# Last block: sixteen attention turns of two heads, with the projections between them

## The chip, the cores and the metric

The kernel runs on one core of a Trainium2 chip. The metric is the device time of one execution in microseconds (us); less is better. TensorE (PE) multiplies, VectorE (DVE) and ScalarE (ACT) work elementwise, GpSimd (POOL) helps, SyncE (SP) issues the weight loads.

## The reference, cut to what matters

The model is a stack of four blocks and then a last block of another kind, on one sequence of 512 positions with 1024 features. Only the last block is touched. It has four mixers side by side, each of 256 features in 4 heads of 64:

```python
def forgetting_attention(q, k, v, log_f):
    ...
        logits = (jnp.einsum('bhqd,bhkd->bhqk', qb, k) * scale
                  + cb[..., None] - cum[:, :, None, :])
        logits = jnp.where(key_pos[None, :] <= q_pos[:, None], logits, -jnp.inf)
        return jnp.einsum('bhqk,bhkd->bhqd', jax.nn.softmax(logits, axis=-1), v)

def stick_breaking_attention(q, k, v):
    ...
        log_keep = jnp.where(mask, jax.nn.log_sigmoid(-z), 0.0)
        log_rest = lax.cumsum(log_keep, axis=3, reverse=True) - log_keep
        att = jnp.where(mask, jnp.exp(jax.nn.log_sigmoid(z) + log_rest), 0.0)
```

The third mixer is a linear recurrence with a 64x64 state per head (`rwkv7_time_mix`), the fourth a gated linear unit (`rg_lru`). Each result is multiplied by its gate, all four are put together and projected (`w_out`).

## The kernel before

Everything is in float32. A product with weights is made of three matmuls over rounded high and low parts (`gemm`). Weights come in units of 128x2048: SyncE loads a unit, ScalarE rounds its high part (`high`), VectorE makes the low part (`low`, an operation of 2.3 us), and TensorE uses 16 tiles of it. There are two raw and three rounded buffers.

Each engine has an order written out by hand, and engines meet by semaphores. Long chains (the recurrence) are generators in the list `bgs`: each call of `bg()` lets an engine do one more step of them, up to the next `yield`, at a place that is the same in the orders of all engines. `rwkv_tensor`, `rwkv_vector`, `rwkv_scalar`, `rwkv_gpsimd` hold these steps for a pair of heads (`pp`): preparation (decay, keys, bonus), four 64x64 products of chunks, four transposed tiles, five levels of a triangular inverse (a "split" product and two "crossed" ones each), three products more, a state loop of 8 chunks with two steps each, and a normalisation at the end. Half a step more or less on one engine is waited for by the others.

PSUM has eight banks: four in the ring `gb` for projections, values and attention outputs, four in `mb` for scores, transposes and all products of the recurrence. `take` gets the next bank that isn't held and waits until its last content was read.

The attention (`attend_tensor`, `attend_scalar`, `attend_vector`, `attend_others`; kind 0 forgetting, kind 1 stick-breaking) goes for each kind: the values of four tiles, then for each of two pairs of heads the q and the k projection (`proj_tensor`, 24 matmuls of 512 columns), and then eight scores, one head and one 128-row query tile each, in the order of `SEQ`: 512, 512, 384, 384, 256, 256, 128, 128 key columns. `steps` lays these over each other: at a step TensorE transposes the weights of a score two or three back, makes a new score, and multiplies an older one with the values, with a `bg()` behind the score and one behind the product. For kind 0 the score is followed by a second product of 4 rows (line 2669) that adds the negative cumulated forget gates of the keys (`cum`) from a one-hot column of `cst`:

```python
pmm(pe, b, h, b[:, 0:n], q_[r, 128 * x:128 * x + 128], k_[r, 0:n], True, kind == 1)
if kind == 0:
    pmm(pe, b, 2, b[:, 0:n], K.ident[64:68, 64 + hd:65 + hd].broadcast_to([4, 128]), X.cum[64:68, 0:n], False, True)
```

`pmm` counts each product and waits for the last one in the same bank when the row group changes. On VectorE a kind 0 score takes a bias and mask operation on the last 128 columns, a bias on the rest (lines 2788 and 2790), a maximum, its negation, and after ScalarE's exp a reciprocal and a scaling. A kind 1 score takes abs, exp, ln on ScalarE and five operations on VectorE (lines 2812 to 2822), one of them a scan, then a last exp on ScalarE. Between the first and the second pair of kind 0 stands `between`: the recurrence of heads pair 0 is finished, the three projections of pair 1 are made, and its recurrence is begun.

## Time and profile before

| | us |
|---|---|
| median of 3 runs | 3229.66 |
| lowest, highest | 3228.27, 3239.74 |
| the profiled execution | 3230.81 |
| its span, first to last instruction | 3229.0 |
| mean granted TensorE clock | 0.94 of full speed |

Busy shares of the span: TensorE 91%, its weight loads 74%, VectorE 48%, ScalarE 34%, GpSimd 7%. The last block begins near 2740 us, the attention part of it runs from 2846.4 to 3163.6, and then come the last projection, the norm and the output. Busy time of an engine is not time at its peak: a matmul at the lower clock is busy for longer. Matmuls in float32 leave two records each. Tile names in the rows: `hh_`, `hl_` are the block's input, `wh_`, `wl_` weights, `Fg_` holds q, k, values and two score buffers, `rraw_` a third, `R_` the recurrence's tiles, `ST_`, `SA_` its state, `htf_` the transposed weights, `cum_` the cumulated gates, `cst_` the identity, `ps` a PSUM bank.

### The profile page before, as it was taken

The numbers are of one execution on the slowest core, as the hardware profiler recorded it, in microseconds if no ns is written. First come the engines' busy times: TensorE is split into PE (matmuls) and PEld (weight loads), VectorE is DVE, ScalarE is ACT, GpSimd is POOL, SyncE is SP. The second block draws the span as 40 slices with busy tenths as digits, with TensorE's granted clock in tenths as the row PEclk, the third lists the DMA queues.
The fourth block names the chain that finished last, engine by engine and source line by source line (L and its number), as shares of the span: only waits on it lengthen the run. The fifth ranks groups of instructions, "written<-read, shape, count | busy, mean of one in ns | idle before, by whom it ended". The sixth has DMA issues, their size and how long they took to land.

```text
span 3229.0 us, 39111 instructions
## 1 busy us (share of the span) xinstructions
PE 2949.0 (91%) x15982; PEld 2381.0 (74%) x15982; DVE 1552.2 (48%) x2302; ACT 1088.7 (34%) x1665; POOL 235.3 (7%) x216
## 2 busy tenths in 40 slices
PE   6999997399999989989999799998999998898977
PEld 5787886377888787787787488887788886665745
DVE  5776763834434334534334554344543344534444
ACT  4332332343212225525445232222332223422233
POOL 2333220000000000000000300000100000100000
PEclk9999998799999989989999899999999999987868
DMA  3244547433443221121221322222122222111000
GB/s 112 88 146 154 169 128 233 165 121 105 130 118 117 78 98 53 53 96 65 82 82 69 131 92 98 98 91 79 66 92 104 92 92 86 53 40 40 15 26 27
DMA packets 109956, 305.40 MB, mean 95 GB/s; under 512 B 27488, under 2 KB 67872, under 8 KB 80464
## 3 DMA queue, kind: packets, MB, share of 16 engines
q1 hardware_dynamic: 104656, 281.40, 26.3%
q10 hardware_dynamic: 5120, 21.50, 1.8%
q8 instruction: 125, 2.05, 0.3%
q14 instruction: 55, 0.45, 0.0%
HBM read 265.20 MB, written 41.85 MB: 95 GB/s over the span
## 4 chain that ended last, share of the span: by engine, by line
PE 80%; DVE 8%; ACT 3%; issue 2%; POOL 1%; SPq 1%; DMA 1%; DVEq 0%; ACTq 0%; POOLq 0%
PE ps L94 79%; DVE s_ L121 2%; PE ps L99 1%; SPq L158 1%; DVE H_ L121 1%; DVE htf_ L135 1%; ACT htf_ L117 0%; ACT hh_ L117 0%; ACT wh_ L117 0%; DVE ol_ L121 0%; DVE Pm_ L121 0%; ACT R_ L117 0%; ACT PT_ L117 0%; DVE nmx_ L143 0%; DVE R_ L121 0%
## 5 line engine op out<-in xcount | busy, mean ns | idle before, releaser
L94 PE MATMUL ps<-hh_,wh_ 128*128 128x512 f32 x2184 | 869.3, 398 | 20.4 <-DVE hl_ L121 12.4
L94 PE MATMUL ps<-hl_,wh_ 128*128 128x512 f32 x2184 | 854.6, 391 | 0.0
L94 PE MATMUL ps<-hh_,wl_ 128*128 128x512 f32 x2184 | 854.1, 391 | 0.0
L121 DVE TENSOR_TENSOR wl_<-raw_,wh_ 128x2048 fp32r<-128x2048 f32 x209 | 480.5, 2299 | 548.1 <-ACT wh_ L117 548.1
L117 ACT ACTIVATE wh_<-raw_ 128x2048 fp32r<-128x2048 f32 x209 | 399.0, 1909 | 354.6 <-PE ps L94 339.7
L94 PEld LDWEIGHTS ps<-hh_,wh_ 128*128 128x128 f32 x2184 | 412.7, 189 | 120.8 <-DVE hl_ L121 11.1
L94 PEld LDWEIGHTS ps<-hh_,wl_ 128*128 128x128 f32 x2184 | 412.5, 189 | 87.7
L94 PEld LDWEIGHTS ps<-hl_,wh_ 128*128 128x128 f32 x2184 | 413.2, 189 | 86.5 <-issue 3.7
L94 PE MATMUL ps<-ah_,wl_ 128*128 128x512 f32 x704 | 279.5, 397 | 0.0
L94 PE MATMUL ps<-ah_,wh_ 128*128 128x512 f32 x704 | 278.3, 395 | 0.0
L94 PE MATMUL ps<-al_,wh_ 128*128 128x512 f32 x704 | 277.7, 395 | 0.0
L117 ACT ACTIVATE sg_<-sg_ 128x512 f32<-128x512 f32 x88 | 55.6, 632 | 305.2 <-DVE sg_ L121 305.1
L94 PEld LDWEIGHTS ps<-ah_,wh_ 128*128 128x128 f32 x704 | 132.1, 188 | 32.7 <-issue 1.3
L94 PEld LDWEIGHTS ps<-al_,wh_ 128*128 128x128 f32 x704 | 132.1, 188 | 32.5
L94 PEld LDWEIGHTS ps<-ah_,wl_ 128*128 128x128 f32 x704 | 132.0, 188 | 31.5
L94 PE MATMUL ps<-wh_,hh_ 128*128 128x256 f32 (+1 forms) x480 | 141.4, 295 | 14.6 <-POOL hl_ L121 8.7
L121 DVE TENSOR_TENSOR sg_<-sg_,ps 128x512 f32<-128x512 f32 x88 | 60.5, 688 | 171.1 <-PE ps L94 130.4
L94 PE MATMUL ps<-wl_,hh_ 128*128 128x256 f32 (+1 forms) x480 | 139.1, 290 | 0.0
L94 PE MATMUL ps<-wh_,hl_ 128*128 128x256 f32 (+1 forms) x480 | 139.0, 289 | 0.0
L117 ACT ACTIVATE ah_<-sg_ 128x512 fp32r<-128x512 f32 x88 | 55.6, 632 | 238.9 <-DVE sg_ L121 238.9
L121 DVE TENSOR_TENSOR x_<-x_,ps 128x512 f32<-128x512 f32 x96 | 65.7, 685 | 143.2 <-PE ps L94 143.2
L117 ACT ACTIVATE sq_<-x_ 128x512 f32<-128x512 f32 x70 | 44.2, 632 | 239.8 <-DVE x_ L121 231.8
(318 smaller groups left out, 3696.1 us busy)
## 6 DMA issues: line engine op xcount, KB each, us to landing
raw_<-in_w SPq DMA_DIRECT2D x209, 1024.0 KB, 4.9
sO<-s5ce_ SPq DMA_DIRECT2D x32, 256.0 KB, 3.7
sW<-s5wt_ SPq DMA_DIRECT2D x16, 512.0 KB, 3.8
sA<-os_ SPq DMA_DIRECT2D x24, 256.0 KB, 2.2
ol_<-sA SPq DMA_DIRECT2D x24, 256.0 KB, 3.6
sT<-sK SPq DMA_DIRECT2D x32, 128.0 KB, 3.4
wh_<-sO ACTq DMA_DIRECT2D x4, 1024.0 KB, 11.3
wl_<-sO ACTq DMA_DIRECT2D x4, 1024.0 KB, 13.1
```

The source lines that it names most:

```text
L94: return self.e.matmul(out, lhsT, rhs, start=start, stop=stop, skip_group_check=True)
L99: return self.e.transpose(out, a, ident)
L117: return self.e.activation(out, a, f, bias=bias, scale=scale)
L121: return Nothing() if self.e is None else self.e.tensor_tensor(out, a, b, op)
L135: return self.e.scalar_tensor_tensor(out=out, in0=a, scalar=s, in1=b, op0=op0, op1=op1)
L158: return Nothing() if self.e is None else self.e.dma_start(out, a)
```

## The change

- Both heads of a pair go together. There are 16 turns (4 pairs i by 4 query tiles, 512 to 128 columns) and three more to run dry. In turn t TensorE makes the products of turn t-3 (the two heads alternate over key blocks, to column halves 0 and 64 of the bank), the transposes of turn t-2, and two scores one behind the other (row halves 0 and 64, two banks), then one `bg()`, then `FILLS[t]` pieces of projections, then two `bg()`.
- The pieces are half a q or k projection (12 matmuls) or one value tile (24 matmuls of 256 columns): 16 of them in turns 0 to 11. Only the first values and the first pair's q and k stand ahead of the turns.
- `between` (three projections) stands at turn 4, the recurrence of pair 1 gets its steps from turn 4 on.
- The 4-row product behind each score is gone. Instead four broadcasts of a whole row of `cum` (4 rows, 512 columns) are made once, ScalarE copies them to SBUF (`four`: the tiles `sq0`, `sq1`, `rs`, `ssq`), and VectorE adds score, query's gate and key's gates in one operation over all columns, and the mask in a second one over 128 columns.
- VectorE does, in a turn: both heads' score operations, both heads' scaling (kind 0), one `bg()`, at turns 6, 10, 14, 18 the gating of a finished pair, the fill's part (weights' low part, k copy), two `bg()`. ScalarE: two copies of transposes, both heads' exp (or abs, exp, ln), `bg()`, in kind 1 the last exp of the turn before, fill, two `bg()`.
- In kind 1 both scores of a turn are held in their banks until the next turn (`hold=i > 1`).
- The q and k tiles have two buffers each, score buffers number four. The weight units of the last block are laid out in the new order of use. Three tiles that only the first stages use are given free.
- In `rwkv_vector` four `yield`s, one behind each of four evacuations, become two behind each second one.

The diff, cut to its core:

```diff
--- before.py
+++ after.py
         dv.mark("out", "r.m", pp, n)
-        yield
+        if n % 2:
+            yield
+            yield
     yield
...
+TURNS = 16
+FILLS = (1, 1, 1, 1, 1, 1, 1, 2, 1, 1, 2, 3) + (0,) * 7
+V_ORDER = (0, 1, 2, 3), (3, 2, 1, 0)
...
 def at_views(K):
...
+    q = [Fg[:, 0:512], X.lw[:, :, :].rearrange("p a b -> p (a b)")]
+    k = [Fg[:, 516:1028], X.k1[:, :]]
...
-    Pm = [Fg[:, 2056:2056 + 512], Fg[:, 2568:2568 + 512], X.raw[:, 0:512]]
+    Pm = [Fg[:, 2056:2056 + 512], Fg[:, 2568:2568 + 512], X.cum[:, :], X.Pm3[:, :]]
+    four = [K.sq[0][:, :], K.sq[1][:, :], K.rs[:, :], K.ssq[:, :]]
...
-    return Fg[:, 0:512], Fg[:, 516:1028], V, Pm, [K.sq[0], K.sq[1], K.rs], neg
+    return q, k, V, Pm, four, neg
+def turn(t, h):
+
+    x = 3 - t % 4
+    return 2 * t + h, t // 4, x, 128 * (x + 1), 2 * (t % 2) + h
+def fill(e, t):
+    for _ in range(FILLS[t]):
+        next(e.fills)
...
-                pmm(pe, b, h, b[:, 0:n], q_[r, 128 * x:128 * x + 128], k_[r, 0:n], True, kind == 1)
-                if kind == 0:
-                    hd = 2 * pp + h
-                    pe.wait_ge(*K.at("f.ncu"))
-                    pmm(pe, b, 2, b[:, 0:n], K.ident[64:68, 64 + hd:65 + hd].broadcast_to([4, 128]), X.cum[64:68, 0:n], False, True)
-                pe.mark("aS", q0 + score)
-                pe.bg()
...
+def heads_tensor(K, pe, i):
+
+    for name in ("pr.q", "pr.k"):
+        b = K.gb.take(name, i, hold=True)
+        pe.wait_ge(*K.after(pe, K.gb, name, i))
+        for ks in (range(4), range(4, 8)):
+            gemm_part(K, pe, b, lambda k: (K.hh[:, k, :], K.hl[:, k, :], ("h", 8, k)), 8, ks)
+            if ks[0]:
+                pe.mark(name, i)
+                pe.rows.pop(id(b), None)
+                K.gb.let(name, i)
+            yield
+def fills_of(K, e, heads, values):
+
+    yield from heads(K, e, 1)
+    yield from heads(K, e, 2)
+    yield from values(K, e, 1)
+    yield from heads(K, e, 3)
+def attend_tensor(K, pe, between):
+    X = K.mx
+    q_, k_, V, Pm, four, _ = at_views(K)
+    for hd in range(4):
+        b = take(K, pe, K.mb, "f.b", hd)
+        pe.wait_ge(*K.at("f.ncu"))
+        pe.mm(b, K.ident[64:68, 64 + hd:65 + hd].broadcast_to([4, 128]), X.cum[64:68, :], True, True).then_inc(*pe.up("f.b", hd))
+    for _ in values_tensor_2(K, pe, 0):
         pe.bg()
+    for _ in heads_tensor(K, pe, 0):
         pe.bg()
+    pe.fills = fills_of(K, pe, heads_tensor, values_tensor_2)
+    for t in range(TURNS + 3):
+        if t == 4:
+            between()
+        if 3 <= t:
+            i, n = turn(t - 3, 0)[1], (t - 3) % 4
+            if n == 0:
+                O = take(K, pe, K.gb, "aO", i, hold=True)
+            for h in range(2):
+                pe.wait_ge(*K.at("a2.PT", turn(t - 3, h)[0]))
+            pe.wait_ge(*K.at("out", "av", i // 2, 3))
+            x = turn(t - 3, 0)[2]
+            for kk in range(x + 1):
+                for h in range(2):
+                    c = 64 * (2 * (i % 2) + h)
+                    pmm(pe, O, 0, O[64 * h:64 * h + 64, 128 * x:128 * x + 128], V[:, kk, c:c + 64],
+                        K.htf[h][:, 128 * kk:128 * kk + 128], kk == 0, kk == x)
+            pe.mark("a2.w", t - 3)
+            if n == 3:
+                pe.mark("aO", i)
+                K.gb.let("aO", i)
+        if 2 <= t < TURNS + 2:
+            for h in range(2):
+                q, i, x, n, w = turn(t - 2, h)
+                b = take(K, pe, K.mb, "aT", q)
+                pe.wait_ge(*K.at("a2.P", q))
                 for kk in range(x + 1):
+                    m = pe.tr(b[:, 128 * kk:128 * kk + 128], Pm[w][:, 128 * kk:128 * kk + 128], K.ident)
+                m.then_inc(*pe.up("aT", q))
+        if t < TURNS:
+            if t > 8:
+                for h in range(2):
+                    K.mb.let("aS", turn(t - 1, h)[0])
+            for h in range(2):
+                q, i, x, n, w = turn(t, h)
                 r = slice(64 * h, 64 * h + 64)
+                b = take(K, pe, K.mb, "aS", q, hold=i > 1)
+                pe.wait_ge(*K.at("a2.q", i))
+                pe.wait_ge(*K.at("a2.k", i))
+                pe.mm(b[:, 0:n], q_[i % 2][r, 128 * x:128 * x + 128], k_[i % 2][r, 0:n], True, True).then_inc(*pe.up("aS", q))
+        elif t == TURNS:
+            for h in range(2):
+                K.mb.let("aS", turn(TURNS - 1, h)[0])
+        pe.bg()
+        fill(pe, t)
+        pe.bg()
+        pe.bg()
...
+def attend_scalar(K, ac, between):
+    X = K.mx
+    q_, k_, V, Pm, four, _ = at_views(K)
+    for hd in range(4):
+        ac.wait_ge(*K.at("f.b", hd))
+        ac.wait_ge(*K.at("y", 6))
+        ac.wait_ge(*K.at("y", 7))
+        ac.act(four[hd], K.mb["f.b", hd], ACT.Copy).then_inc(*ac.up("out", "f.b", hd))
+    for _ in values_scalar_2(K, ac, 0):
+        ac.bg()
+    for _ in heads_scalar(K, ac, 0):
+        ac.bg()
+    ac.fills = fills_of(K, ac, heads_scalar, values_scalar_2)
+
+    def sticks_end(t):
+        for h in range(2):
+            q, i, x, n, w = turn(t, h)
+            ac.wait_ge(*K.at("a2.lg", q))
+            ac.act(Pm[w][:, 0:n], Pm[w][:, 0:n], ACT.Exp).then_inc(*ac.up("a2.P", q))
+
+    for t in range(TURNS + 3):
+        if t == 4:
             between()
+        if 2 <= t < TURNS + 2:
+            for h in range(2):
+                q, i, x, n, w = turn(t - 2, h)
                 ac.wait_ge(*K.at("aT", q))
+                if t > 2:
+                    ac.wait_ge(*K.at("a2.w", t - 3))
+                ac.act(K.htf[h][:, 0:n], K.mb["aT", q][:, 0:n], ACT.Copy).then_inc(*ac.up("a2.PT", q))
                 ac.mark("out", "aT", q)
+        if t < TURNS:
+            for h in range(2):
+                q, i, x, n, w = turn(t, h)
+                if i < 2:
+                    ac.wait_ge(*K.at("a2.mx", q))
+                    ac.act(Pm[w][:, 0:n], Pm[w][:, 0:n], ACT.Exp, bias=X.rp[:, w:w + 1], accum=X.rp[:, 4 + w:5 + w]).then_inc(*ac.up("a2.ex", q))
+                else:
+                    e1 = four[w][:, 0:n]
                     ac.wait_ge(*K.at("aS", q))
+                    ac.wait_ge(*(K.at("a2.e1", q - 4) if q > 19 else K.at("a2.mx", 15)))
                     ac.act(e1, K.mb["aS", q][:, 0:n], ACT.Abs).then_inc(*ac.up())
                     ac.wait_ge(*ac.now())
                     ac.act(e1, e1, ACT.Exp, scale=-1.0).then_inc(*ac.up())
                     ac.wait_ge(*ac.now())
                     ac.act(e1, e1, ACT.Ln, bias=1.0).then_inc(*ac.up("a2.ln", q))
+        ac.bg()
+        if 8 < t <= TURNS:
+            sticks_end(t - 1)
+        fill(ac, t)
+        ac.bg()
+        ac.bg()
...
+def attend_vector(K, dv, between):
...
+    for _ in values_vector_2(K, dv, 0):
         dv.bg()
+    for _ in heads_vector(K, dv, 0):
         dv.bg()
+    dv.fills = fills_of(K, dv, heads_vector, values_vector_2)
+    for t in range(TURNS + 3):
+        if t == 4:
             between()
+        for h in range(2) if t < TURNS else ():
+            q, i, x, n, w = turn(t, h)
+            p, dg, b = Pm[w], slice(128 * x, n), K.mb["aS", q]
+            if i < 2:
+                hd = 2 * i + h
+                dv.wait_ge(*K.at("aS", q))
+                dv.wait_ge(*K.at("out", "f.b", 3))
+                if q > 3:
+                    dv.wait_ge(*K.at("aT", q - 4))
+                dv.stt(p[:, 0:n], b[:, 0:n], X.cq[:, x, hd:hd + 1], four[hd][:, 0:n], ALU.add, ALU.add).then_inc(*dv.up("out", "aS", q))
+                dv.wait_ge(*dv.now())
+                dv.tt(p[:, dg], p[:, dg], NEGC, ALU.add).then_inc(*dv.up())
+                dv.wait_ge(*dv.now())
+                dv.red(X.rp[:, w:w + 1], p[:, 0:n], ALU.max).then_inc(*dv.up())
+                dv.wait_ge(*dv.now())
+                dv.ts(X.rp[:, w:w + 1], X.rp[:, w:w + 1], -1.0, None, ALU.mult).then_inc(*dv.up("a2.mx", q))
+            else:
+                e1 = four[w][:, 0:n]
+                dv.wait_ge(*K.at("a2.ln", q))
+                dv.stt(e1, b[:, 0:n], 0.0, e1, ALU.max, ALU.add).then_inc(*dv.up())
+                dv.wait_ge(*dv.now())
+                dv.tt(e1[:, dg], e1[:, dg], ONS, ALU.mult).then_inc(*dv.up())
+                dv.wait_ge(*K.at("aT", q - 4))
+                dv.wait_ge(*dv.now())
+                dv.scan(p[:, 0:n][:, ::-1], K.ones[:, 0:1].broadcast_to([128, n]), e1[:, ::-1], 0.0,
+                        ALU.mult, ALU.subtract).then_inc(*dv.up("a2.e1", q))
+                dv.wait_ge(*dv.now())
+                dv.tt(p[:, 0:n], p[:, 0:n], b[:, 0:n], ALU.add).then_inc(*dv.up("out", "aS", q))
+                dv.wait_ge(*dv.now())
+                dv.tt(p[:, dg], p[:, dg], NEGS, ALU.add).then_inc(*dv.up("a2.lg", q))
+        for h in range(2) if t < 8 else ():
+            q, i, x, n, w = turn(t, h)
+            dv.wait_ge(*K.at("a2.ex", q))
+            dv.recip(X.rp[:, 4 + w:5 + w], X.rp[:, 4 + w:5 + w]).then_inc(*dv.up())
+            dv.wait_ge(*dv.now())
+            dv.ts(Pm[w][:, 0:n], Pm[w][:, 0:n], X.rp[:, 4 + w:5 + w], None, ALU.mult).then_inc(*dv.up("a2.P", q))
+        dv.bg()
+        if t > 3 and t % 4 == 2:
+            i = (t - 3) // 4
+            dv.wait_ge(*K.at("aO", i))
+            gated(K, dv, i, K.gb["aO", i])
+            dv.mark("out", "aO", i)
+        fill(dv, t)
+        dv.bg()
+        dv.bg()
+def attend_gpsimd(K, po, between):
+    for _ in range(8):
+        po.bg()
+    for t in range(TURNS + 3):
+        if t == 4:
+            between()
+        for _ in range(3):
+            po.bg()
...
+    sqk = qk(sq, sk)
     return np.concatenate([_units(_tiles(np.concatenate([low, rkv(0), lx], 1))), _units(_tiles(np.concatenate([fg, sg, rg, lg], 1))),
-                           v(fv), qk(fq, fk)[0:1], _units(_tiles(rkv(1))), qk(fq, fk)[1:2], v(sv), qk(sq, sk)])
+                           v(fv), qk(fq, fk), _units(_tiles(rkv(1))), sqk[0:1], v(sv), sqk[1:2]])
```

## Rows read from the trace of the kernel before

**Rows 1.** Windows view, stretches of the attention part: length, then busy us (instructions) per engine, clock, DMA.
```profile
core 0: us, PE busy (x) PEld busy (x) DVE busy (x) ACT busy (x) POOL busy (x), PEclk, DMA share, GB/s
2846.40:2882.40 36.00, 35.28 (x309) 29.78 (x309) 8.95 (x16) 6.82 (x9) 0.00 (x0) 0.91 0.17 59
2882.40:2938.20 55.80, 47.22 (x190) 25.22 (x188) 20.81 (x65) 12.30 (x30) 0.64 (x2) 0.59 0.00 1
2938.20:2957.00 18.80, 18.80 (x74) 15.32 (x74) 6.11 (x5) 3.56 (x3) 0.00 (x0) 0.87 0.16 57
2957.00:2985.50 28.50, 17.81 (x121) 11.73 (x119) 15.79 (x22) 11.10 (x14) 3.15 (x3) 0.88 0.21 74
2985.50:3043.10 57.60, 55.09 (x780) 39.47 (x780) 26.87 (x66) 14.50 (x37) 6.34 (x5) 0.82 0.01 2
3043.10:3077.00 33.90, 32.15 (x234) 26.57 (x233) 9.29 (x18) 5.43 (x7) 0.00 (x0) 0.95 0.17 62
3077.00:3126.00 49.00, 35.19 (x154) 20.40 (x153) 24.52 (x56) 20.49 (x45) 0.00 (x0) 0.55 0.00 1
3126.00:3137.90 11.90, 11.08 (x48) 8.84 (x48) 3.67 (x3) 1.89 (x2) 0.00 (x0) 1.00 0.23 88
3137.90:3163.60 25.70, 17.80 (x76) 10.59 (x76) 18.61 (x40) 16.94 (x40) 0.00 (x0) 0.73 0.00 1
```

**Rows 2.** Groups of instructions by form, 2846 to 3163.5, TensorE: the 4-row products.
```profile
L94 PE MATMUL ps<-cum_,cst_ 4*128 4x512 f32 x8 | 6.6, 914 | 0.2
```

**Rows 3.** Timeline, TensorE: start us, us, instruction; scores and 4-row products.
```profile
2882.39 1.12 PE L94 MATMUL ps<-Fg_ 64*128 64x512 f32 x2
2883.57 1.12 PE L94 MATMUL ps<-cum_,cst_ 4*128 4x512 f32 x2
...
2885.19 2.07 PE L94 MATMUL ps<-Fg_ 64*128 64x512 f32 x2
...
3137.96 1.74 PE L94 MATMUL ps<-Fg_ 64*128 64x512 f32 x6 [0.87 <-DVE Fg_ L139]
```

**Rows 4.** Timeline, TensorE: products with the values, and transposes.
```profile
2912.46 1.97 PE L94 MATMUL ps<-htf_,Fg_ 128*64 128x128 f32 x8
...
3001.17 0.60 PE L99 MATMUL ps<-cst_,rraw_ 128*128 128x128 f32 x4
...
3014.86 1.09 PE L94 MATMUL ps<-htf_,Fg_ 128*64 128x128 f32 x8
```

**Rows 5.** Timeline, TensorE: the recurrence's chunk products; crossed x64, split x32 at 3022.15.
```profile
2980.00 0.69 PE L94 MATMUL ps<-R_ 64*64 64x64 f32 x32 [0.62 <-DVE R_ L121]
...
3018.82 2.38 PE L94 MATMUL ps<-R_ 64*64 64x64 f32 x64
...
3022.15 1.15 PE L94 MATMUL ps<-R_ 64*64 64x64 f32 x32
```

**Rows 6.** Timeline, VectorE: first and last of a kind 0 and a kind 1 score, one scaling.
```profile
2884.73 0.35 DVE L135 SCALAR_TENSOR_TENSOR Fg_<-ps,cq_,c_ 128x128 f32<-128x128 f32 x1 [1.94 <-PE ps L94]
...
2886.36 0.15 DVE L128 TENSOR_SCALAR rp_<-rp_ 128x1 f32<-128x1 f32 x1
...
2997.04 0.49 DVE L128 TENSOR_SCALAR rraw_<-rraw_,rp_ 128x512 f32<-128x512 f32 x1
...
3141.04 0.69 DVE L135 SCALAR_TENSOR_TENSOR sq_<-ps,sq_ 128x512 f32<-128x512 f32 x1 [3.23 <-ACT sq_ L117]
...
3144.07 0.29 DVE L121 TENSOR_TENSOR Fg_<-Fg_,c_ 128x128 f32<-128x128 f32 x1
```

**Rows 7.** Timeline, ScalarE: exp of a kind 0 score; exp and ln of kind 1.
```profile
2887.84 0.72 ACT L116 ACTIVATE Fg_<-Fg_,rp_ 128x512 f32<-128x512 f32 x1
...
3139.72 1.29 ACT L117 ACTIVATE sq_<-sq_ 128x512 f32<-128x512 f32 x2
```

**Rows 8.** Timeline, VectorE: last multiplications of the preparation; two state steps.
```profile
2977.26 2.69 DVE L121 TENSOR_TENSOR R_<-R_ 128x512 f32<-128x512 f32 x4
...
3044.89 0.28 DVE L135 SCALAR_TENSOR_TENSOR SA_<-ps,R_ 64x128 f32<-64x128 f32 x1 [1.29 <-PE ps L94]
...
3045.70 0.21 DVE L121 TENSOR_TENSOR ST_<-ST_,ps 128x64 f32<-128x64 f32 x1
```

More of the change, by code:

```diff
@@ L2832, in attend_others @@
-def attend_others(K, e, kind, proj, between=None):
-    for t in range(4):
-        e.bg()
-        if t == 0 and proj is proj_sync:
-            load(K, e, e.unit + 3)
-    e.unit += 1
-    for pp in range(2):
-        for _ in range(2):
-            proj(K, e) if proj is proj_sync else proj(e)
-            e.bg()
-        for turn, score, finish, weigh in steps(kind, pp):
-            if score is not None:
-                e.bg()
-            if weigh is not None:
-                e.bg()
-        if between and pp == 0:
+        if t == 3:
+            dv.unit += 1
@@ L2849, in attend_others @@
             between()
+        fill(sp, t)
 def drain(e):
@@ L3372, in memory @@
         fourier_memory(K, st, 3)
+    first.close()
     X = K.mx = Place()
```

284 lines of the change are left out of this document (83 added, 201 removed).

## The prediction

> **What bounds the kernel now.** I read the page first: TensorE is busy for 91% of the span, but only the last block is touched. So I read the windows view, cut at the ends of the steps of the attention part [rows 1]. It lasts from 2846.4 to 3163.6, 317.2 us. The reader is to see three things there. In the stretches of values and projections (2846 to 2882, 2938 to 2957, 3043 to 3077, 3126 to 3138) TensorE is full and its clock is 0.87 to 1.00, so they can only move, not shrink. In the four attention stretches (55.8, 57.6, 49.0 and 25.7 us, 188 us together) the clock is 0.55 to 0.82 and other engines end the waits. From 2957.0 to 2985.5 the recurrence of heads pair 1 runs its serial preparation on VectorE and ScalarE, and TensorE is busy for 17.8 of 28.5 us. The change spreads three things over 16 turns: attention, q/k/v projections, recurrence steps. The question is whether a turn is shorter than what it replaces.
>
> **TensorE's part.** Removed: 16 forget-bias products. The four of 512 columns show 6.6 us [rows 2]; by columns the four widths make 6.6 x (1 + 0.75 + 0.5 + 0.25) = 16.5 us. Each also waits for the score before it: score to bias starts 1.18 us apart for 1.12 us of work at 2.4 GHz [rows 3]. Added: four such broadcasts at the start, back to back, 4 us.
> Scores pair up. Three scores of different row halves (512, 512, 384 columns) once stood together and took 1.74 us, while one alone takes 1.12 us, 2.07 at 1.2 GHz [rows 3]. By that a pair of 512 takes about 1.0 us instead of 2.3. The products are one head after the other now, eight records in 1.09 us (1.97 at 1.2 GHz) [rows 4]. No row shows 128x64 products of two column halves alternating. Bounds: no overlap (1.0 us per four key blocks and head, nothing gained) and full overlap (half). The nearest row is the recurrence's 64x64 products, where 32 records that use all four quadrants take 0.69 us and 64 that use two at a time 2.38 us [rows 5]: column halves do overlap. I take half. Four transposes take 0.60 us [rows 4], unchanged.
> At 2.4 GHz a turn thus has on TensorE, for 512 columns: products 0.9, transposes 1.2, scores 1.1. Over the four widths of a head pair: 2.3 + 2.4 + 2.4 = 7.1 us. A half projection is 12 matmuls, 2.75 us (48 in 11.1 us in the stretch to 3137.9, at clock 1.00 [rows 1]); a value tile 3.2 us is my estimate from the same view (the 36.0 us stretch less two projections and eight recurrence steps of 1.5, by four).
>
> **VectorE's part, which sets the turn.** In the first eight turns VectorE does both heads' bias, mask, maximum, then waits for ScalarE's exp and scales, and only then serves a recurrence step. From the first operation to the negated maximum it is 1.78 us at 512 columns [rows 6]. The new form (one 512-column operation from PSUM at 0.69, one 128-column at 0.29, instead of 0.35 chained to 0.61) adds 0.15, so 1.9. Both heads 3.8, the second exp and its read-out 1.1 (0.72 for the exp [rows 7]), scaling 0.5 plus reciprocal 0.2 [rows 6]: 5.6 us. For 384, 256, 128: 4.9, 4.2, 3.5. In the last eight, abs/exp/ln of the first head take 1.9 us on ScalarE (0.6 and 1.29 [rows 7]), then VectorE 3.2 us a head (3141.04 to 3144.36 [rows 6]), 6.4 for both, then 5.3, 4.2, 3.1.
> After that come the steps. A state step on VectorE and back is 0.8 us (3044.89 to 3045.70) plus 0.5 for the update [rows 8]. Two of a turn's three steps come after VectorE's attention, because TensorE's second needs VectorE's answer to the first: 2.2 us. The projection half hides under the attention on VectorE, as long as that takes over 2.75 us. So turn = products + transposes + scores + VectorE's attention + 2.2.
>
> **The sum**, in us, part by part:
> - Start: 36.0 [rows 1] + 4.0 for the broadcasts, which stand ahead of the values on TensorE: 40. Cover for ScalarE's four copies: the values.
> - Turns 0 to 3: 1.1+5.6+2.2, 0.8+4.9+2.2, 1.8+4.2+2.2, 2.3+3.5+2.2 = 33, + 2.3 for a weight cast in a fill ahead of the second step, + 3 for the recurrence's last mean and variance (two round trips), + 2 for TensorE at 1.2 GHz part of the time: 40. Two projections are inside.
> - Three recurrence projections at turn 4: 19 [rows 1].
> - Turn 4: the preparation. Now it takes from 2957.0 to the end of the last of four multiplications at 2979.95 [rows 8], 23.0 us, with projections under it. VectorE's attention for turn 4 now stands in the middle, 5.6, and the first products' evacuation follows, 1.4: 30.
> - Turn 5: 8. Turn 6: products, transposes, scores 2.1, the recurrence's 16 transposes 2.0, fill 2.75, product 1.15, two evacuations 1.4, split 1.15, evacuation 0.8, crossed 2.38 [rows 5]: 13.7, + 2 for low clock: 16.
> - Turn 7 (two fills): 2.4 + 1.15 + 5.9 + 2.4 + 0.9 + 1.15 = 14. Turn 8: 1.4 + 1.1 + 1.9 + 6.4 + 1.4 + 1.15 + 0.8 + 2.4 = 17. Turn 9: 12. Turn 10 (two fills, three products of 3.5) 14. Turn 11 (three fills, 8.2) 14: here TensorE sets the turn, not VectorE.
> - Turns 12 to 15, no fill: 14 + 11.5 + 10.4 + 9.2 = 45, + 5 for low clock: 50. End: 10.
> Sum 40+40+19+30+8+16+14+17+12+14+14+50+10 = 284, against 317.2: **-33 us**. Hidden and costed at nothing: SyncE's eight loads (same bytes, DMA share at most 0.23 [rows 1]), the moved yields in `rwkv_vector` (four before, four after), GpSimd's steps (same), the new tiles (memory of finished stages). If that cover went, a late load would show as ScalarE's cast waiting for a DMA.
> The profiled execution is 3230.8 us (span 3229.0); less 33 is 3197.6. The median of the three runs is 1.2 lower, so I say **3196**. A measurement of this kernel can tell about 0.5%, 16 us, from no change.
>
> **The range.** Fast ends (turn 4's attention overlaps ScalarE's parts, clock full): 39+35+17+26+6+13+12+14+10+12+12+43+8 = 247, which is 3160. Slow ends (clock 1.2 GHz in most turns): 24 more, see below, 3220; I go to 3226.
>
> **Rivals.**
> A, low clock. TensorE's clock is 0.59 and 0.55 in the stretches where only small products run, 1.00 in dense projections [rows 1]; after the stretch at 0.59 the next one begins low, at 0.87 in the mean. If a half projection per turn does not lift it, two groups' 7.1 us and the recurrence products of turns 6 to 10 (some 20 us, half as much again) cost 14 + 10 = 24 more: 3220, no measurable change. Against it: 2985 to 3043 kept 0.82 without any projection. The Trainium skill (TensorE: Matmul & The Clock Gate, HAM oscillation) says that dense bursts parted by waits each begin at the lower clock, and advises keeping dense work together; this change parts 16 pieces that now stand together, so by that page the time is this rival's. The rows above agree that a dense stretch behind a sparse one begins low.
> B, better overlap. The engines' orders leave more slack than my turn formula (fills take the round trips, VectorE's second head starts while TensorE transposes): 37 us less, 3160.
> C, pairing is only in the text: products and scores of two heads still run one after the other. Then 9.6 us of scores and 8.5 of products return, about 15 of it on the chain: 3211. Against: [rows 3, 5].
> D, slower. In the last eight turns two of the four small PSUM banks are held by the scores for a whole turn, so transposes, products and steps share two. If the first step of each turn then waits for a bank that is emptied only behind VectorE's attention, the fill is no longer covered (3.2 + 3.2 + 5.9 + 8.2 = 20), one more round trip comes per turn (8 x 1.8 = 14), the recurrence's products come on top (7), at low clock (12): 53 more, 3249. It decides once turns 5 to 15, which I have at 13.2 us in the mean, pass 17.7. Against: now, with three scores held, a state step at 3077 to 3126 passes between them.
>
> **Chances.** My forecast 0.52 (nearly all of it below 3213.5), A 0.17, B 0.18, C 0.07 (half below), D 0.06. Faster by over 0.5%: 0.50 + 0.18 + 0.04 = 0.72; within: 0.22; slower: 0.06.
>
> **What would show it.** Right: no product of `cum_` beside scores; score pairs of 512 columns starting within 0.1 us and done in about 1 us; product pairs in half the time; the loop of 19 turns with the three projections from the first score to the last product about 244 us; turn 4 the longest, with TensorE idle behind VectorE; turns 7, 10, 11 full on TensorE. Wrong: turns of equal length whatever the width (something else than VectorE's attention sets them), ScalarE waiting for weights, or TensorE waiting in `take` for a bank in turns 8 to 15.

## The result, and the profile after

The kernel after takes 3221.83 us (median of 8 runs, 3219.05 to 3226.67), the kernel before 3232.66 us (8 runs, 3228.27 to 3239.74): ratio 0.9968, 95% interval 0.9957 to 0.9979, 10 us less. The profiled execution has a span of 3218.3 us against 3229.0. Faster, but by 0.3%, where 1% was forecast.

One thing has to be said before small differences are read. All kernels of this study do the same work in their first 2840 us, and yet in the profiled executions the last 4x4 product of `cum_`, just ahead of the attention part, starts anywhere between 2842.5 and 2852.5 us. So beside the medians I give the **rest**: from that product to the end of the span. It is 383.2 us before (2845.74 to 3228.99) and 372.3 after (2845.97 to 3218.31): 10.9 less, all of it behind that product.

The windows view of after, cut at the starts of turns (first scores of turns 0, 4, 5, 7, 10, 11, 12 and 15), the columns as in [rows 1]:

```profile
core 0: us, PE busy (x) PEld busy (x) DVE busy (x) ACT busy (x) POOL busy (x), PEclk, DMA share, GB/s
2846.60:2889.00 42.40, 40.94 (x318) 31.53 (x318) 8.98 (x16) 9.21 (x13) 0.00 (x0) 0.88 0.14 51
2889.00:2948.00 59.00, 48.75 (x279) 35.21 (x278) 31.27 (x74) 18.01 (x31) 0.64 (x2) 0.88 0.12 41
2948.00:2982.10 34.10, 14.28 (x100) 8.07 (x98) 19.73 (x32) 12.08 (x18) 2.43 (x3) 0.70 0.14 53
2982.10:3007.30 25.20, 22.35 (x275) 18.07 (x274) 12.92 (x32) 7.37 (x19) 3.21 (x3) 0.86 0.01 2
3007.30:3055.20 47.90, 36.21 (x519) 31.05 (x518) 24.94 (x45) 16.35 (x34) 3.96 (x3) 0.86 0.07 23
3055.20:3078.20 23.00, 16.68 (x182) 13.81 (x180) 8.50 (x17) 7.77 (x16) 0.00 (x0) 0.85 0.13 46
3078.20:3092.60 14.40, 13.28 (x84) 9.92 (x84) 4.86 (x15) 3.58 (x11) 0.00 (x0) 0.95 0.00 1
3092.60:3136.90 44.30, 22.23 (x148) 14.09 (x148) 19.68 (x45) 13.71 (x30) 0.00 (x0) 0.54 0.00 1
3136.90:3153.30 16.40, 10.48 (x59) 5.79 (x58) 6.17 (x17) 6.97 (x20) 0.00 (x0) 0.62 0.00 0
```

The part lasts 306.7 us against 317.2. TensorE is nearly full at the start and in turns 5, 6, 7 and 11 (turn 7 alone: 12.18 of 13.4 us, clock 1.00); in turn 4 and in turns 12 to 14 it is busy for half the time or less, and the clock there is 0.70 and 0.54. The parts of the sum beside what they became (start of a turn: its first scores; the last column is the best kernel of this study):

| part | forecast | after | E12 |
|---|---|---|---|
| start | 40 | 42.4 | 40.9 |
| turns 0 to 3 and three projections | 59 | 59.1 | 54.0 |
| turn 4 | 30 | 34.1 | 28.5 |
| turn 5, 6, 7 | 8, 16, 14 | 6.8, 18.4, 13.4 | 9.3, 18.3, 10.7 |
| turn 8, 9 | 17, 12 | 19.9, 14.6 | 17.9, 11.0 |
| turn 10, 11 | 14, 14 | 22.9, 14.5 | 18.7, 13.7 |
| turns 12 to 15 and end | 60 | 60.6 | 42.5 |
| sum | 284 | 306.7 | 265.5 |

What the change does to single operations, from the timeline of TensorE after:

```profile
2847.34 5.69 PE L94 MATMUL ps<-cum_,cst_ 4*128 4x512 f32 x8 [1.15 <-DVE cum_ L128]
2918.29 1.09 PE L94 MATMUL ps<-htf_,Fg_ 128*64 128x128 f32 x16
2948.04 1.13 PE L94 MATMUL ps<-k_,lw_ 64*128 64x512 f32 x4
3074.79 1.97 PE L94 MATMUL ps<-htf_,Fg_ 128*64 128x128 f32 x16
3092.64 2.08 PE L94 MATMUL ps<-k_,lw_ 64*128 64x512 f32 x4
```

The four broadcasts cost 5.7 us and a wait of 1.15. Pairing is real: two heads' products, 16 records, take 1.09 us (1.97 at half clock), what 8 records of one head took before [rows 4]; two heads' scores of 512 columns take 1.13 (2.08), what one took [rows 3]. But the 8 records of before stood alone: when the same 16 go one head after the other without a pause, they take 1.58 us (E6), so alternating takes a third off them, not half.

How a late turn is spent, from the timeline of turn 12 after, all three engines in order of time, lines left out at the dots:

```profile
3092.64 2.08 PE L94 MATMUL ps<-k_,lw_ 64*128 64x512 f32 x4
3094.65 0.33 PE L94 MATMUL ps<-SA_,R_ 64*64 64x64 f32 x4
3094.75 0.60 ACT L117 ACTIVATE sq_<-ps 128x512 f32<-128x512 f32 x1 [1.73 <-PE ps L94]
3096.70 0.69 DVE L135 SCALAR_TENSOR_TENSOR sq_<-ps,sq_ 128x512 f32<-128x512 f32 x1 [5.75 <-ACT sq_ L117]
...
3103.32 0.21 DVE L121 TENSOR_TENSOR ST_<-ST_,ps 128x64 f32<-128x64 f32 x1
3103.56 0.28 DVE L135 SCALAR_TENSOR_TENSOR ST_<-ST_,pc_,R_ 128x64 f32<-128x64 f32 x1
3103.90 0.90 PE L94 MATMUL ps<-R_,ST_ 64*64 64x64 f32 x3 [8.64 <-DVE ST_ L135]
3105.52 0.29 DVE L135 SCALAR_TENSOR_TENSOR SA_<-ps,R_ 64x128 f32<-64x128 f32 x1 [1.67 <-PE ps L94]
3106.42 0.22 DVE L121 TENSOR_TENSOR ST_<-ST_,ps 128x64 f32<-128x64 f32 x1 [0.61 <-PE ps L94]
```

The products of the first step end at about 3095.3. VectorE stands idle 5.75 us for ScalarE, then does both heads' attention, and answers the step at 3103.3; TensorE has waited 8.64 us. Only then come steps two and three, and the next turn's scores stand behind them.

### The profile page after: what moved, and what is told of

It reads as the page before. It is cut to its first block, busy times and chain, and to the rows that moved or that the text cites. A ratio compares the mean times of both kernels' runs of the same rounds, so it can differ in the third digit from the quotient of the medians.

```text
span 3218.3 us, 39085 instructions
## 1 busy us (share of the span) xinstructions
PE 2904.1 (90%) x15958; PEld 2360.8 (73%) x15958; DVE 1555.4 (48%) x2306; ACT 1091.1 (34%) x1669; POOL 236.3 (7%) x216
## 4 chain that ended last, share of the span: by engine, by line
PE 79%; DVE 9%; ACT 4%; issue 2%; POOL 1%; SPq 1%; DMA 0%; DVEq 0%; ACTq 0%; POOLq 0%
PE ps L94 78%; DVE s_ L121 1%; PE ps L99 1%; SPq L158 1%; DVE htf_ L135 1%; DVE H_ L121 1%; ACT htf_ L117 1%; ACT wh_ L117 1%; DVE R_ L121 0%; ACT hh_ L117 0%; DVE Pm_ L121 0%; DVE wl_ L121 0%; ACT rs_ L117 0%; DVE ol_ L121 0%; DVE Fg_ L135 0%
## 6 DMA issues: line engine op xcount, KB each, us to landing
wl_<-sO ACTq DMA_DIRECT2D x4, 1024.0 KB, 13.9
```

## The experiments

Theory 1: a turn is a chain through VectorE, long because of what stands in its line ahead of a recurrence step (the attention, weight casts), and the gain of the change lies elsewhere. Rivals: TensorE's work or low clock sets the turns; pairing and order bring the gain. In the table stand the median, the ratio to the kernel before with its 95% interval, the rest in the profiled execution, and the loop, which goes from the first scores to the last value product. E7 has the edits of E2 and E5 together, and E9 to E12 build on it:

| run | median | ratio | rest | loop |
|---|---|---|---|---|
| after | 3221.8 | 0.9968 (0.9957 to 0.9979) | 372.3 | 264.3 |
| E1 late cast | 3221.3 | 0.9966 (0.9953 to 0.9978) | 372.1 | 262.3 |
| E2 steps first | 3197.1 | 0.9887 (0.9868 to 0.9905) | 348.6 | 239.8 |
| E3 fills in turn 4 | 3229.0 | 0.9981 (0.9972 to 0.9991) | 375.8 | 267.1 |
| E4 bias alone | 3219.3 | 0.9964 (0.9951 to 0.9976) | 372.9 | |
| E5 fills last | 3216.3 | 0.9960 (0.9947 to 0.9974) | 367.5 | 258.7 |
| E6 unpaired | 3226.6 | 0.9986 (0.9977 to 0.9995) | 377.8 | 269.1 |
| E7 both orders | 3195.6 | 0.9890 (0.9876 to 0.9904) | 341.6 | 235.0 |
| E8 dense work in waits | 3222.4 | 0.9976 (0.9964 to 0.9988) | 371.8 | 262.6 |
| E9 fills in waits | 3193.2 | 0.9874 (0.9857 to 0.9892) | 345.1 | 236.4 |
| E10 all steps first | 3197.5 | 0.9897 (0.9881 to 0.9914) | 346.5 | 238.1 |
| E11 one step first | 3186.3 | 0.9860 (0.9842 to 0.9878) | 338.1 | 230.0 |
| E12 all together | 3182.0 | 0.9842 (0.9823 to 0.9861) | 331.4 | 224.6 |

### E4: the bias alone, in the old order

The edit, cut to its core (ScalarE's four copies and the waits are left out):

```diff
@@ attend_tensor of before, kind 0, ahead of the values
+        for hd in range(4):
+            b = take(K, pe, K.mb, "f.b", hd)
+            pe.mm(b, K.ident[64:68, 64 + hd:65 + hd].broadcast_to([4, 128]), X.cum[64:68, :], True, True)...
@@ the scores
-                pmm(pe, b, h, b[:, 0:n], q_[...], k_[r, 0:n], True, kind == 1)
-                if kind == 0:
-                    pmm(pe, b, 2, b[:, 0:n], K.ident[...], X.cum[64:68, 0:n], False, True)
+                pmm(pe, b, h, b[:, 0:n], q_[...], k_[r, 0:n], True, True)
@@ attend_vector
-                    dv.stt(w[:, dg], b[:, dg], c, NEGC, ALU.add, ALU.add)
-                    dv.ts(w[:, 0:128 * x], b[:, 0:128 * x], c, None, ALU.add)
+                    dv.stt(w[:, 0:n], b[:, 0:n], c, four_of(K)[hd][:, 0:n], ALU.add, ALU.add)
+                    dv.tt(w[:, dg], w[:, dg], NEGC, ALU.add)
```

> The kernel before, with one part of the change alone: the forget bias by four broadcasts ahead of the values and an add of VectorE, the 16 forget-bias products gone; the order of work is as before. Theory 1 (part of what the change removes had not been on the path): the broadcasts cost their full 6 us at the start, where TensorE is full, and the removed products give back 5 to 10 of their 16.5 us: between 0 and 4 us less than before. Rival (the scores' products are on the path): 16.5 less 6 and 2.4 for VectorE's longer form, 8 us less than before. Second rival (all of it was covered): 6 to 8 us more than before.

Measured 3219.3 us, 10.3 less than before by the rest: as much as the whole change. Windows of its two attention stretches of the first kind:

```profile
2898.20:2945.00 46.80, 37.14 (x175) 21.91 (x173) 22.31 (x67) 12.35 (x30) 0.64 (x2) 0.58 0.00 0
2992.20:3041.00 48.80, 43.72 (x764) 34.60 (x764) 28.05 (x68) 14.39 (x37) 6.35 (x5) 0.90 0.01 2
```

They were 55.8 and 57.6 us [rows 1]: 9.0 and 8.8 less. The start, from the last 4x4 product to the first scores, grows from 36.7 to 45.8, and the stretch behind the second (3041.0 to 3073.4) is 1.5 shorter: together 10.2. (In E4 the broadcasts meet the half clock, 6.83 us, and the clock of the start is 0.85 against 0.91.) In the kernel before, the removed products keep TensorE busy for 10.2 and 8.3 us in these two stretches, 18.5 in all, part of them at half clock. 17.8 us came off, so they were almost wholly on the path (the clock of the second stretch also rose from 0.82 to 0.90, and no run parts its share). The first rival was right, and my middle guess of 5 to 10 us was too low. The other parts of the change (16 turns, pairing, projections between the turns) together gave nothing that can be measured: 0.6 us by the rest, and E4 is the faster by 2.6 us in the medians and by 2.2 in the rest too, once the start is taken out (45.8 us there, 43.0 after, for the lower clock).

### E6: pairing undone

```diff
-            for kk in range(x + 1):
-                for h in range(2):
+            for h in range(2):
+                for kk in range(x + 1):
```

> The kernel after, with the value products of a turn one head after the other (as before the change) instead of alternating. The traces show 16 records in 1.39 us paired, 8 in 1.09 of one head at 2.4 GHz, so unpaired they take 0.8 us more at four key blocks and 8 us more over the 16 turns on TensorE. Theory 1 (the chain of a turn goes through VectorE, with products ahead of the scores on it): all of it is on the path, 5 to 8 us more than after, 3228. Rival (products lie in TensorE's slack): within 2 us of after, and the pairing was worth nothing in time.

Two groups of value products of this run, at the full and at half clock:

```profile
2917.46 1.58 PE L94 MATMUL ps<-htf_,Fg_ 128*64 128x128 f32 x16
3077.40 2.85 PE L94 MATMUL ps<-htf_,Fg_ 128*64 128x128 f32 x16
```

Measured 5.5 us more by the rest, 4.8 by the medians: as theory 1 expects. The 16 groups of value products take 22.0 us of TensorE in sum, 16.9 in the kernel after, and the loop is 4.8 longer: they are on the path. The saving stands where a turn has four or three key blocks (16 records: 1.58 us unpaired, 1.09 paired; 12: 1.15 and 0.88); with two and one it is nothing (1.13 and 1.12, 0.44 and 0.44). Pairing the products is worth some 5 us, known to within a few (the intervals of E6 and after just touch). Since everything but the bias came to nothing measurable, the order of the 16 turns must have cost about as much as pairing gave, or somewhat more; that last step is a difference, not a run of its own.

### E2: two steps ahead of the attention, turns 8 to 15

```diff
+EARLY = range(8, 19)
@@ TensorE
         pe.bg()
+        if t in EARLY:
+            pe.bg()
         fill(pe, t)
@@ ScalarE and VectorE, ahead of the attention
+        if t in EARLY:
+            dv.bg()
+            dv.bg()
```

(and one step behind it instead of three; the gating of a pair's output stands ahead of the two steps, since a step takes its bank)

> The kernel after, in turns 8 to 15 with the first two of a turn's three recurrence steps ahead of the attention on VectorE and ScalarE (TensorE: both ahead of the fill). Theory 1 (the late steps set the turn): the two round trips fall into the 5 us in which VectorE waits for abs, exp and ln, and the next scores no longer wait for VectorE; turns 8 to 15 fall from 14 to 23 us each to 10 to 18, 20 us less in all, 3202. Rival (a turn is VectorE's and ScalarE's own work, or TensorE at low clock, whatever the order): within 3 us of the kernel after, 3219 to 3225.

Measured 3197.1: 24.7 us less than after by the medians, 23.7 by the rest. The turns became 17.2, 13.3, 18.2, 13.7, 10.7, 11.5, 9.5 and 13.9, 108.0 us against 132.5. This is the largest single effect found. The steps now run while ScalarE does abs, exp and ln; the timeline of turn 12 in this run:

```profile
3085.52 1.13 PE L94 MATMUL ps<-k_,lw_ 64*128 64x512 f32 x4 [0.25 <-ACT htf_ L117]
3086.99 0.22 DVE L121 TENSOR_TENSOR ST_<-ST_,ps 128x64 f32<-128x64 f32 x1 [2.79 <-PE ps L94]
3088.75 0.29 DVE L135 SCALAR_TENSOR_TENSOR SA_<-ps,R_ 64x128 f32<-64x128 f32 x1 [1.23 <-PE ps L94]
3089.08 0.69 DVE L135 SCALAR_TENSOR_TENSOR sq_<-ps,sq_ 128x512 f32<-128x512 f32 x1
...
3095.55 0.21 DVE L121 TENSOR_TENSOR ST_<-ST_,ps 128x64 f32<-128x64 f32 x1
3095.80 0.28 DVE L135 SCALAR_TENSOR_TENSOR ST_<-ST_,pc_,R_ 128x64 f32<-128x64 f32 x1
3095.82 0.47 PE L99 MATMUL ps<-cst_,Pm_ 128*128 128x128 f32 x1 [4.68 <-DVE ST_ L121]
```

VectorE answers the step 1.5 us after the scores began (10.7 in the kernel after), and its attention begins 3.6 us after them (4.1 there). The last line is a new wait, taken up in E10.

### E1 and E5: the weight casts

E1 moves one cast, that of turn 10, from the fill to the end of turn 16. E5 leaves each in its turn, but puts all of a fill's work on ScalarE and VectorE behind the third step:

```diff
-        fill(dv, t)
         dv.bg()
         dv.bg()
+        fill(dv, t)
```

> The kernel after, with one weight cast moved: the one that ScalarE and VectorE do inside turn 10's fill is done at the end of turn 16. Theory 1 (VectorE serves its steps too late): in turn 10 TensorE's fill is over when ScalarE starts the cast (3068.05), and VectorE's answer to the step waits for both halves of the cast, until 3072.28; without it turn 10 falls from 22.9 to about 18.5 us, 4 us less in all, 3218. Rival (TensorE's two fills and its clock set turn 10): turn 10 stays within 1 us, 3221 to 3222.

> The kernel after, with what ScalarE and VectorE do in a fill (weight casts, evacuations of q and k and of the values) behind all three recurrence steps of the turn instead of between them; TensorE's order as it was. Theory 1 (what stands ahead of a step on VectorE lengthens the turn): turn 10 loses the 3.5 us that the late cast gave, turn 4 the same (the cast stands between the preparation's steps at 2965.9 to 2970.1), turn 7 one to two; turn 11, whose third half projection is awaited by the next scores, gains 1 back: 7 us less than after, 3215. Rival (the casts only take the place of waits for TensorE): within 2 us of after.

Turn 10 in the kernel after, from the timelines of VectorE, TensorE and ScalarE:

```profile
3062.38 0.68 DVE L121 TENSOR_TENSOR G_<-G_,ps 128x512 f32<-128x512 f32 x1
3063.11 0.39 PE L94 MATMUL ps<-wh_,hh_ 128*128 128x256 f32 x1 [2.46 <-DVE G_ L121]
3068.05 1.91 ACT L117 ACTIVATE wh_<-raw_ 128x2048 fp32r<-128x2048 f32 x1
3069.99 2.29 DVE L121 TENSOR_TENSOR wl_<-raw_,wh_ 128x2048 fp32r<-128x2048 f32 x1 [6.94 <-ACT wh_ L117]
3072.25 0.11 DVE L155 MEMSET ST_<- 128x64 f32 x1
3072.50 0.62 PE L94 MATMUL ps<-R_,ST_ 64*64 64x64 f32 x3 [2.04 <-DVE ST_ L155]
```

The cast's slot comes free with TensorE's last value product, in the same fill; ScalarE casts at 3068.05, VectorE ends its half at 3072.28, and the zero state that the first state step needs is set behind it. Taking the cast away gives TensorE's 2.04 us of wait and 1.5 more, which goes with the clock: in the kernel after it falls to 0.50 behind that wait (3074.1 to 3077.2), in E1 it stays at 1.00, and the turn's last 16 products take 1.09 us in place of 1.97. In E1 turn 10 fell from 22.9 to 19.4 us (18.5 expected), but 3.3 us came back at the end: 1.5 in the last turns, since the cast now stood in ScalarE's line ahead of the last transposed weights (TensorE waits 1.94 us for them in place of 0.46), and 1.8 behind the last value product, where the output projection begins 0.8 us later and runs at the lower clock for longer (0.59 in its first 7 us, against 0.75). The whole gave nothing. A right mechanism, and a miss for the time. In E5 turn 4 fell from 34.1 to 30.5, turn 10 to 19.4, turn 11 by 0.8 where a loss was expected, and turns 12 to 15 by 1.7; turn 7, from which one to two were expected, kept its length (13.7 against 13.4), and turn 5 grew by 1.2. In all 4.8 us less by the rest, 5.5 by the medians, 7 expected. Turn 0 lost 1.3 and turns 1 to 3 gave 3.3 back, the latter not for their code: E7, with the same there, hasn't lost it (last section).

### E3 and E9: half projections into turn 4

E3 fills turn 4 with four halves behind the first step, on all engines; E9 does it on top of E7's orders, with TensorE's halves parted:

```diff
-FILLS = (1, 1, 1, 1, 1, 1, 1, 2, 1, 1, 2, 3) + (0,) * 7
+FILLS = (1, 1, 1, 1, 4, 0, 0, 1, 1, 1, 2, 3) + (0,) * 7
@@ E9 only, TensorE in turn 4: two halves, step, half, step, half, step
```

> The kernel after, with the three half projections of turns 5, 6 and 7 done in turn 4, where TensorE waits 8.9, 6.3 and 3.4 us for the recurrence's preparation (fills 4, 0, 0, 1 in place of 1, 1, 1, 2). Theory 1: turns 5 to 7 are set by VectorE's attention plus the steps behind it, so a fill is nearly covered there; turn 4 grows by at most 1 us, turns 5 to 7 lose 1 us each: 2 us less, 3220. Rival (TensorE's work sets turns 5 to 7, and its clock): the three halves, 2.75 us each and more at half clock, come off the path: 7 to 9 us less, 3214.

> Both orders of the run before this one, and the three half projections of turns 5 to 7 moved into turn 4 again, but TensorE does two ahead of the first step, one behind it and one behind the second, and ScalarE and VectorE evacuate behind the third. Theory 1 (the same move lost 3.4 us because VectorE stood 4.56 us before an evacuation with the preparation behind it; TensorE's own waits of 8.9, 2.9 and 3.4 us have room): turn 4 stays at 29.8 within 1 us and turns 5 to 7 lose 3 us as they did there: 3 us less from the last 4x4 product to the end (341.6 there). Rival (TensorE's added work sets turn 4 itself): turn 4 grows by 3 us or more and nothing is won.

E3 was slower than after, by 3.4 us in the rest and by 7.2 in the medians: both theories missed. Turns 5 to 7 lost 3.1 us in sum, turn 4 grew by 4.9. From its timeline:

```profile
2980.92 0.69 DVE L139 COPY Fg_<-ps 128x512 f32<-128x512 f32 x1 [4.56 <-PE ps L94]
2981.53 0.68 DVE L121 TENSOR_TENSOR R_<-R_ 128x512 f32<-128x512 f32 x1
```

VectorE waits 4.56 us for the fourth half, with the recurrence's preparation behind it in its line. That is theory 1's own mechanism, which I had failed to apply. In E9, with the evacuation behind the steps, turn 4 stays at 29.5 and turns 4 to 9 are 4.1 us shorter in sum than in E10, which has the same turns 0 to 3, and 3.1 shorter than in E7: expected 3. By the rest E9 stands 3.5 us above E7 all the same, and by the medians 2.4 below: in E7's profiled execution the start and turns 0 to 3 together are 5.4 us shorter, with the same code.

### E7, E10, E11, E12: how far the order goes

> The two edits of order together: in turns 8 to 15 two steps ahead of the attention, and in all turns the fills of ScalarE and VectorE behind the third step. Theory 1: the gains add where they meet different turns (turn 4's 3.5 and turn 7's 1 to 2 come on top of the 24 us of the first edit; turn 10's 3.5 as well, as it is still 18.2 us long): 7 us less than with the first edit alone, 3190. Rival (the first edit has already taken what the casts cost): 3194 to 3198.

The loop lost 4.8 us more than in E2, the rest 7.0, the median 1.5: the median lies in the rival's range, not at 3190. Turn by turn both had a part. Turn 4 fell by 4.3 us as theory 1 expects, but turn 10 (18.2 in E2, 18.7 here) and turn 7 gave nothing, which is what the rival says. A size can't be told to the microsecond: E7's profiled execution was the fastest of its four (3188.6; the others 3195.3 to 3199.7), and its first five turns take 87.0 us where E10, with the same code in them, shows 91.6. This bears on every comparison with E7 below.

E10 puts the third step of turns 12 to 15 ahead too (`AHEAD` 3 in place of 2), E11 one step ahead in turns 0 to 3 and 5 to 7 (`AHEAD` 1 in place of 0), both on E7.

> Both orders, and in turns 12 to 15 all three steps ahead of the attention in place of two. In the run with both orders TensorE waits 4.30 us for VectorE's last step, before the second head's transposes of turn 13: they need the PSUM bank that the third step's product holds until VectorE, behind its attention, has read it. Theory (bank wait): it goes, and turns 12 to 14 lose 1.5 to 2.5 us each, 5 us less from the last 4x4 product to the end, 336.6. Rival (VectorE's attention, 5.3 to 6.4 us a turn with what stands around it, sets these turns; a third round trip ahead of it only delays it): within 1.5 us of 341.6.

> Both orders, and in turns 0 to 3 and 5 to 7 one step ahead of the attention on ScalarE and VectorE. Theory 1: one of the two late round trips of a turn goes, 0.5 to 1 us in each of the seven turns, 5 us less from the last 4x4 product to the end, 336.6. Rival (in these turns there is no wait for abs, exp and ln that the step could fill, so that the attention starts later by what the step takes, and turns 5 to 7 have steps of 1 to 2.4 us on TensorE): within 1.5 us of 341.6, or more.

E10: turn 12 falls from 10.7 to 6.1 us, and the wait for the bank is gone:

```profile
3088.60 0.68 DVE L135 SCALAR_TENSOR_TENSOR sq_<-ps,sq_ 128x512 f32<-128x512 f32 x1
3089.37 0.48 PE L99 MATMUL ps<-cst_,cum_ 128*128 128x128 f32 x1
3089.64 0.42 PE L99 MATMUL ps<-cst_,Pm_ 128*128 128x128 f32 x1
3090.21 2.44 PE L94 MATMUL ps<-k_,lw_ 64*128 64x384 f32 x3 [0.15 <-ACT htf_ L117]
```

But turns 14 and 15 grow by 1.2 and 1.9, and the four lose only 1.8 in sum: the wait was real, its removal mostly only showed that VectorE's own work is next. The expected 5 us did not come; E10 is 1.9 us slower than E7 in the medians and 4.9 in the rest, of which 4.6 lie in the first five turns. E11: 3186.3, 9 us under E7's median, 5.0 in the loop, 3.6 in the rest. Most of it is in turn 3 (27.9 to 23.7), where VectorE ends the first pair's recurrence 9.7 us into the turn in place of 13.9, and the three projections follow sooner; the single turns 0, 2 and 6 lost 0.6 to 1.1, turns 4 and 5 grew by as much. Right in the total, wrong in the place, and with a size that isn't firm: E12, the same code in turns 0 to 3, takes 54.0 us for them where E11 takes 51.6 and E7 57.2.

> All edits of order together: fills of ScalarE and VectorE behind the third step; on ScalarE and VectorE one step ahead of the attention in turns 0 to 3 and 5 to 7, two in turns 8 to 11, three in turns 12 to 15; the half projections of turns 5 to 7 in TensorE's waits of turn 4. Theory 1 (each takes out waits of its own): from the run with one step first (230.0 us from the first scores to the last value product) 4.0 off for turns 5 to 9 and 1.7 for turns 12 to 15, 224 us, and a median of 3180 to 3182. Rival (the one step first in turns 5 to 7 and the emptied turns 5 and 6 take the same wait twice): 228 to 230, 3185 to 3187.

3182.0, loop 224.6, as expected: the gains add. It is 40 us faster than the kernel after and 51 faster than the kernel before, with the change's tiles and operations and another order of them alone.

### E8: is it the clock?

```diff
         fill(pe, t)
+        if 12 <= t < 16:
+            d = take(K, pe, K.gb, "idle", t)
+            for k in range(12):
+                m = pe.mm(d, K.hh[:, k % 8, 0:128], K.hh[:, k % 8, :], k == 0, k == 11)
+            m.then_inc(*pe.up("out", "idle", t))
```

> The kernel after, with 12 dense products of 512 columns whose result nobody reads put into each of turns 12 to 15 behind the first step, where TensorE waits 8.6, 6.1, 5.5 and 3.5 us for VectorE. Rival A (TensorE's low clock, 0.5 of full from 3108.9 on, lengthens the turns): the clock rises, turns 13 to 15 and the end get 4 to 8 us shorter although work is added. Theory 1 (these turns wait for VectorE and ScalarE): the added products lie in the wait and the turns stay within 0.5 us of 16.0, 14.4, 13.9 and 16.3, or the last grows by 1 to 2 where the wait is only 3.5; the clock may rise all the same.

Windows of turns 12, 13, 14 and of turn 15 with the end; first after, then this run:

```profile
3092.60:3108.70 16.10, 6.72 (x48) 3.67 (x48) 7.50 (x15) 4.76 (x11) 0.00 (x0) 0.61 0.00 0
3108.70:3123.10 14.40, 7.77 (x46) 4.82 (x46) 6.22 (x14) 4.71 (x10) 0.00 (x0) 0.50 0.00 1
3123.10:3136.90 13.80, 7.74 (x59) 5.60 (x58) 5.96 (x16) 4.24 (x10) 0.00 (x0) 0.50 0.00 1
3136.90:3153.30 16.40, 10.48 (x59) 5.79 (x58) 6.17 (x17) 6.97 (x20) 0.00 (x0) 0.62 0.00 0
```

```profile
3095.50:3111.40 15.90, 9.56 (x58) 5.80 (x58) 7.49 (x15) 4.68 (x11) 0.00 (x0) 0.71 0.00 0
3111.40:3125.70 14.30, 11.90 (x56) 7.84 (x56) 6.21 (x14) 4.79 (x10) 0.00 (x0) 0.62 0.00 1
3125.70:3139.20 13.50, 12.09 (x73) 8.80 (x72) 5.95 (x16) 4.24 (x10) 0.00 (x0) 0.63 0.00 1
3139.20:3154.40 15.20, 12.50 (x71) 7.79 (x70) 6.13 (x17) 6.75 (x19) 0.00 (x0) 0.81 0.00 1
```

The clock rises from 0.50 to 0.62 in turns 13 and 14 and from 0.62 to 0.81 at the end; the four lose 1.7 us in all, 1.1 of it at the end, more than theory 1 allowed there and less than half of what rival A asked. The low clock is no more than a small part of what sets these turns; the run doesn't bring it to 1.00, so its whole price isn't shown. The dense work is hidden in the waits.

## Why the prediction was wrong, point by point

The sign and the range held; 33 us were forecast, 10 to 11 came. The mechanism was right (VectorE's attention with the steps behind it sets a turn). Two parts of the sum came out to the microsecond, and that is partly luck: of turns 12 to 15 with the end, 60 forecast and 60.6 measured, turns 12 to 14 took 44.3 us against 35.9 and a share of the 5 for low clock, and turn 15 with the end 16.3 against 19.2 and the rest of those 5; in turn 12 the two steps behind VectorE's attention took 3.4 us (3103.32 to 3106.76), not 2.2. Turns 0 to 3 with the projections took 59.1 against 59. The step that failed is **the sum of the turns that hold a fill or the preparation: the weight casts, a fill's waits and the recurrence's products at half clock were put at nothing or too low there**. It makes 20.9 of the 22.7 us by which the whole sum was too low:

- **Turn 10, "two fills, three products of 3.5", 14 us: 22.9.** 8.9 us, the largest. The weight cast, which I had counted for turns 0 to 3 alone (2.3), stands in VectorE's line ahead of the first state step: 3.5 by E1 and E5. TensorE's fill moreover waits 2.46 us in `take` until VectorE, behind its attention, has gated the pair's output and freed a bank (the sign that I had set for being wrong), and 0.73 us for ScalarE before that; and the fill, one value tile and one half projection, takes 7.35 us (3063.11 to 3070.46, clock 0.76 up to 3070), not 5.95. Together 8.1 of the 8.9.
- **Turn 4, 30: 34.1.** The same cast, between two steps of the preparation (2965.9 to 2970.1). Without it 30.5 (E5), as forecast.
- **Turns 8 and 9, 29: 34.5, and turn 6, 16: 18.4.** I had taken the crossed products at 2.38 us [rows 5]; in turn 6 they take 4.00, in turns 8 and 9 4.00 and 3.67, after TensorE has waited 4.84 (with a split product in between) and 4.03 us for VectorE. Here rival A has a part of the truth, about 3 us in turns 8 and 9. E2 took 4.0 off the two turns.
- **Start, 40: 42.4.** The broadcasts take 5.69 us and 1.15 of wait, not 4.
- Turn 5, 7, 11 and the rest: 0.6 us less than forecast.

What I had removed from TensorE was near the truth: 16.5 us of forget-bias products, 18.5 in the trace, with next to nothing hidden (E4: 17.8 in the two stretches). Pairing I had at half price, a saving of 8.5 us on the products; it is real, so rival C falls, but E6 shows 5. One sum of the working is wrong in itself: 1.2 us of transposes and 1.1 of scores at 512 columns make 3.0 and 2.75 over the four widths, not 2.4 and 2.4, so the 7.1 us that rival A builds on is 8.0. The wrong belief was one level up: that the new order shortens the chain. E4 shows the same time with the old order. The Trainium skill (Perfetto Trace Analysis, Optimization Strategy) says that where the busiest engine changes between regimes, interleaving them may improve the time. Here, by E4, interleaving with the chain through VectorE left as it was gave nothing, and by E2 and E12 a better order within each engine's line then took off 25 and 40 us. A forecast of the bias alone, 16.5 less 4 less 2.4, is 10 us, what the whole change measured.

Rival A (low clock, 3220) names the right time for the wrong reason. The Trainium skill (TensorE: Matmul & The Clock Gate, HAM oscillation) says that dense bursts parted by waits begin at the lower clock. The trace agrees (the fill of turn 4 begins at half clock behind a wait of 8.87 us), but with the clock raised in part turns 12 to 15 lose 1.7 us (E8), and with the order mended 18 (60.6 to 42.5), with the work unchanged. In turns 0 to 11 the clock was not tried by an experiment of its own, and stays open as a rival for a few us there; the last section has what executions of the same code show, 2 to 5 us. Rival B (better overlap) is what the change could have been: 3182 in E12. Rival D's mechanism exists, a wait for a PSUM bank that VectorE empties behind its attention, 4.68 us in E2; in the kernel after TensorE waits for the step itself first, and ahead of the transposes of turns 8 to 15 no wait for VectorE over 0.33 us is left.

The marks I had set: the loop was forecast at 244 us and is 264.3; no `cum_` product stands beside scores, pairs take the time of one, and turn 4 is the longest, as forecast. "Turns 7, 10, 11 full on TensorE" held for 7 and 11 (12.18 of 13.4 and 13.28 of 14.4 us), not for 10 (16.68 of 23.0).

## What to carry to other kernels

When independent chains are interleaved by hand, the order within each engine's line is the change: a short operation that another engine waits for goes ahead of the long work, into the time in which this engine itself waits (25 us here), and weight casts and evacuations that nobody needs soon go behind it. Undo the parts one by one before a gain is put down to the largest of them: here a simple removal of products, a small part of the edit, held all of it. And a sum that has one term written without its working deserves distrust at exactly that term.
